# Twelve weight units of three output projections as 512 rows by 512 columns instead of 1024 by 256, in a float32 kernel of three blocks on one Trainium2 core

## The reference

```python
# first block: D_MIX = 1024
x = x + jnp.concatenate([o_gla, o_sgu], axis=-1) @ w_out[l]
h = rmsnorm(x, norm_mlp_g[l])
x = x + jnp.square(jax.nn.relu(h @ w_mlp1[l])) @ w_mlp2[l]
...
# second block: 2048 rows, ALPHA = 2 ** 0.25
mix = jnp.einsum("bse,ed->bsd", jnp.concatenate([y_ssm, y_attn], axis=-1), w_out.astype(h.dtype))
return layer_norm(ALPHA * h + mix, ln_g, ln_b)
...
# third block: 2048 rows
y = jnp.concatenate([y_conv, y_hgrn.astype(y_conv.dtype)], axis=-1)
h = h + y @ w_out[i].astype(y.dtype)
```

## Time and profile before

| | |
|---|---|
| median of 3 runs | 3835.29 us (3835.24 to 3836.01) |
| the profiled execution | 3835.1 us, span 3833.4 us |
| granted TensorE clock, mean over the span | 0.981 |
| TensorE matmuls | 20278, busy 95% of the span |
| VectorE, ScalarE, GpSimd busy | 59%, 45%, 15% |
| transfers | 191.40 MB read, 50.33 MB written, 63 GB/s |

### The profile page before, as it was taken

How to read it: one execution, slowest core, us unless ns; L and a number is a source line. 1 busy time by engine, 2 the same in 40 slices (tenths; PEclk the granted TensorE clock), 3 DMA queues, 4 the chain that set the end, 5 groups by cost and what they waited for, 6 DMA issues and landing times.

```text
span 3833.4 us, 48757 instructions
## 1 busy us (share of the span) xinstructions
PE 3642.6 (95%) x20278; PEld 3052.9 (80%) x20278; DVE 2272.0 (59%) x2931; ACT 1725.2 (45%) x2342; POOL 557.3 (15%) x437
## 2 busy tenths in 40 slices
PE   7999889999998998999999989989999999989998
PEld 6778878888876777777777768978888888778998
DVE  4445354456676766655565663468888878843332
ACT  4333244431124655566766772144555554542132
POOL 0001032200000444400000000012222222200001
PEclk9999999999998999999999999999999999999999
DMA  3012023342212011011111123121111111153111
GB/s 109 23 39 88 24 79 110 110 157 88 92 64 89 23 34 39 12 55 28 34 36 28 33 82 141 34 88 34 44 45 39 55 50 44 34 213 106 45 36 70
DMA packets 227392, 244.87 MB, mean 64 GB/s; under 512 B 10007, under 2 KB 190180, under 8 KB 227172
## 3 DMA queue, kind: packets, MB, share of 16 engines
q1 hardware_dynamic: 222391, 224.92, 18.0%
q10 hardware_dynamic: 4781, 16.84, 1.1%
HBM read 191.40 MB, written 50.33 MB: 63 GB/s over the span
## 4 chain that ended last, share of the span: by engine, by line
PE 81%; DVE 9%; ACT 6%; issue 2%; DMA 1%; POOL 1%; SPq 0%; ACTq 0%; DVEq 0%; POOLq 0%
PE pd L211 65%; PE pq L211 13%; PE pd L366 2%; PE pq L366 1%; DVE t L328 1%; DVE t L3457 1%; DVE t L3465 1%; ACT t L3062 1%; ACT t L320 1%; DVE t L3902 0%; ACT t L552 0%; DVE t L2400 0%; DMA yc_scratch<-t 0%; DVE t L560 0%; DVE t L2074 0%
## 5 line engine op out<-in xcount | busy, mean ns | idle before, releaser
L211 PE MATMUL pd<-t 128*128 128x512 f32 (+2 forms) x15104 | 2894.4, 352 | 50.3 <-DVE t L2592 8.7
L211 PEld LDWEIGHTS pd<-t 128*128 128x128 f32 x15104 | 2402.4, 191 | 482.1 <-issue 96.0
L211 PE MATMUL pq<-t 128*128 128x128 f32 (+5 forms) x3846 | 675.2, 335 | 60.5 <-DVE t L3938 16.7
L211 PEld LDWEIGHTS pq<-t 128*128 128x128 f32 (+2 forms) x3846 | 500.0, 181 | 183.0 <-issue 47.6
L320 ACT ACTIVATE t<-t 128x2048 fp32r<-128x2048 f32 (+3 forms) x133 | 212.6, 1599 | 633.8 <-PE pd L211 597.7
L328 DVE TENSOR_TENSOR t<-t 128x2048 fp32r<-128x2048 f32 (+3 forms) x133 | 257.5, 1936 | 180.8 <-ACT t L320 180.3
L1915 DVE TENSOR_TENSOR t<-pd,t 128x512 f32<-128x512 f32 x256 | 172.8, 689 | 103.3 <-PE pd L211 101.2
L2057 POOL TENSOR_TENSOR t<-t 128x2 f32<-128x2 f32 x8 | 10.5, 1307 | 1261.0 <-DVE t L3302 853.2
L3854 POOL TENSOR_TENSOR t<-t 128x512 f32<-128x512 f32 x56 | 96.4, 1722 | 593.8 <-ACT t L3798 316.6
L3185 DVE COPY t<-pd 128x512 f32<-128x512 f32 x64 | 44.2, 691 | 219.8 <-PE pd L366 219.8
L3465 DVE SCALAR_TENSOR_TENSOR t<-t 128x1024 f32<-128x1024 f32 x120 | 172.3, 1436 | 0.5
(11 more groups left out here) (336 smaller groups left out, 2996.6 us busy)
## 6 DMA issues: line engine op xcount, KB each, us to landing
t<-in_w_in_dram SPq DMA_DIRECT2D x97, 512.0 KB, 4.1
t<-in_w_out_dram SPq DMA_DIRECT2D x20, 1024.0 KB, 5.5
t<-in_w_in_dram SPq DMA_DIRECT2D x16, 1024.0 KB, 5.1
t<-in_w_mlp_dram SPq DMA_DIRECT2D x64, 256.0 KB, 3.4
u_scratch<-t SPq DMA_DIRECT2D x64, 256.0 KB, 2.4
t<-in_w_mlp_dram SPq DMA_DIRECT2D x16, 1024.0 KB, 5.0
t<-u_scratch SPq DMA_DIRECT2D x15, 1024.0 KB, 7.2
t<-in_x_dram SPq DMA_DIRECT2D x16, 512.0 KB, 9.2
```

What stands on the lines that cost most here:

```text
L211: ins = e.matmul(out, l, r, start=(first and j == 0), stop=(last and j == n - 1), skip_group_check=True)
```

## The change

Units 0 and 1 of products 1, o2b and o3c, units 2 and 3 of o2a and all four of o3b become units of 512 rows (`kq`, four blocks k) by 512 columns (`nh`). That makes twelve. In `pe_quarter` a tile is one position tile: 4 blocks k times three matmuls of 512 columns, 12 matmuls, and eight tiles in a unit. The sum over the 1024 rows no longer ends in one bank: the tile of `kq` 0 and the tile of `kq` 1 are each added to X by `dve_quarter`. The unit is still 1 MB and 2048 elements in each partition. In o2b the statistics of column blocks 0 and 1 are both taken after the additions of `kq` 1. `pe_proj` and `dve_proj` go; o2a keeps its unit 1 as it was. The diff is cut where a function goes as a whole.

```diff
     def proj_read(tag):
-        return lambda th: ("proj", tag, 3, 2 * th + 1)
+        return lambda th: ("proj", tag, 3, 4 * th + 3)
...
+    def pe_quarter(e, W, kg, kq, nh, v, tag, n):
+        u = pe_unit(e, W, [(nh * 512, 512)], k0=kg * 8 + kq * 4, k=4)
+        for tt in range(NT):
+            b = e.take(PD, "proj", tag, n, tt)
+            for k in range(4):
+                e.wait_ge(*at["HTh", v, kq * 4 + k, tt // 4])
+                e.wait_ge(*at["HTl", v, kq * 4 + k, tt // 4])
+                ins = mms(e, b[:, :], three(HTh[:, kq * 4 + k, tile(tt)], HTl[:, kq * 4 + k, tile(tt)],
+                                            u.h[:, k, :], u.l[:, k, :]), first=k == 0, last=k == 3)
+            ins.then_inc(*at.inc("pe", "proj", tag, n, tt))
+        pe_done(u)
+
+    def dve_quarter(e, X, nh, tag, n, t4, ready, alpha=None):
+        for tt in (2 * t4, 2 * t4 + 1):
+            o = X[:, tt, half(nh)]
+            b = PD.of("proj", tag, n, tt)
+            e.wait_ge(*at["proj", tag, n, tt])
+            e.wait_ge(*at[ready(tt)])
+            if alpha is None:
+                ins = e.tensor_tensor(o, b[:, :], o, ADD)
+            else:
+                ins = e.scalar_tensor_tensor(o, o, alpha, b[:, :], MUL, ADD)
+            ins.then_inc(*at.inc("dve", "added", tag, n, t4, free=("proj", tag, n, tt)))
+
+    QUARTERS = [(0, 0), (0, 1), (1, 0), (1, 1)]
...
     def pe_proj_led(e, W, kg, v, tag, turned_first=None):
-        for n in range(2):
-            u = pe_unit(e, W, [(n * 256, 256)], k0=kg * 8)
-            for t4 in range(4):
-                tm(e, u, 0, 256, [2 * t4, 2 * t4 + 1], v, "proj", tag, n, t4)
-            pe_done(u)
+        for kq in range(2):
+            pe_quarter(e, W, kg, kq, 0, v, tag, kq)
...
     def dve_norm_led(e, X, XN, v, tag, ready0, ready, gname, vacant):
-        for n in range(2):
+        for kq in range(2):
             dve_unit(e)
             for t4 in range(4):
-                dve_added(e, X, tag, n, t4, ready0)
+                dve_quarter(e, X, 0, tag, kq, t4, lambda tt: ("added", tag, 0, tt // 2) if kq else ready0(tt))
...
     def pe_sgu(e):
-        for n in range(2):
-            u = pe_unit(e, W, [(n * 256, 256)])
-            for t4 in range(4):
-                tm(e, u, 0, 256, [2 * t4, 2 * t4 + 1], "sgu", "proj", 1, n, t4)
-            pe_done(u)
+        for kq in range(2):
+            pe_quarter(e, W, 0, kq, 0, "sgu", 1, kq)
...
     def dve_out2(e):
-        dve_proj(e, X2, "o2a", lambda tt: ("x2", tt), ALPHA, begun=2, ahead=lambda e: load_b(e, 0))
+        for t4 in (2, 3):
+            dve_added(e, X2, "o2a", 0, t4, lambda tt: ("x2", tt), ALPHA)
+        dve_unit(e)
+        for t4 in range(4):
+            dve_added(e, X2, "o2a", 1, t4, lambda tt: ("x2", tt), ALPHA)
+        dve_unit(e)
+        for t4 in range(4):
+            dve_quarter(e, X2, 1, "o2a", 2, t4, lambda tt: ("x2", tt), ALPHA)
+        dve_unit(e)
+        for t4 in range(4):
+            if t4 == 2:
+                load_b(e, 0)
+            dve_quarter(e, X2, 1, "o2a", 3, t4, lambda tt: ("added", "o2a", 2, tt // 2))
         load_b(e, 1)
...
         for n in range(2):
             dve_unit(e)
             for p in range(4):
-                added(n, p)
+                dve_quarter(e, X2, 0, "o2b", n, p, lambda tt: ("added", *(("o2b", 0) if n else ("o2a", 3)), tt // 2))
+                if n == 1:
+                    e.wait_ge(*at["added", "o2b", 1, p])
+                    stats(0, p)
+                    stats(1, p)
...
     def pe_out2(e):
-        pe_proj(e, A["w_out_2"][0], 0, "o2a", "o2a", n0=1)
+        u = pe_unit(e, A["w_out_2"][0], [(256, 256)])
+        for t4 in range(4):
+            tm(e, u, 0, 256, [2 * t4, 2 * t4 + 1], "o2a", "proj", "o2a", 1, t4)
+        pe_done(u)
+        for kq in range(2):
+            pe_quarter(e, A["w_out_2"][0], 0, kq, 1, "o2a", "o2a", 2 + kq)
         pe_proj_led(e, A["w_out_2"][0], 1, "o2b", "o2b")
...
     def dve_out3(e):
-        dve_proj(e, X3, "o3b", lambda tt: ("x3", tt), ahead=lambda e: load_c(e, 0))
+        for n, (kq, nh) in enumerate(QUARTERS):
+            dve_unit(e)
+            for t4 in range(4):
+                if (n, t4) == (3, 2):
+                    load_c(e, 0)
+                dve_quarter(e, X3, nh, "o3b", n, t4, lambda tt: ("added", "o3b", n - 2, tt // 2) if kq else ("x3", tt))
...
     def pe_out3(e):
-        pe_proj(e, A["w_out_3"][0], 0, "o3b", "o3b")
+        for n, (kq, nh) in enumerate(QUARTERS):
+            pe_quarter(e, A["w_out_3"][0], 0, kq, nh, "o3b", "o3b", n)
```

More of the change, by code:

```diff
@@ L657, in act_fetch @@
             e.dma(tiles[k][:, :], src[k * 128:(k + 1) * 128, :], name, k)
-    def pe_proj(e, W, kg, v, tag, n0=0):
-        for n in range(n0, 4):
-            u = pe_unit(e, W, [(n * 256, 256)], k0=kg * 8)
-            for t4 in range(4):
-                tm(e, u, 0, 256, [2 * t4, 2 * t4 + 1], v, "proj", tag, n, t4)
-            pe_done(u)
+    def pe_quarter(e, W, kg, kq, nh, v, tag, n):
[21 more added lines that the diff above has]
+    QUARTERS = [(0, 0), (0, 1), (1, 0), (1, 1)]
     LED = [(2, 0), (2, 1), (3, 0), (3, 1), (2, 2), (2, 3), (3, 2), (3, 3)]
     def pe_proj_led(e, W, kg, v, tag, turned_first=None):
-        for n in range(2):
-            u = pe_unit(e, W, [(n * 256, 256)], k0=kg * 8)
-            for t4 in range(4):
-                tm(e, u, 0, 256, [2 * t4, 2 * t4 + 1], v, "proj", tag, n, t4)
-            pe_done(u)
+        for kq in range(2):
+            pe_quarter(e, W, kg, kq, 0, v, tag, kq)
         us = {}
@@ L726, in dve_norm_led @@
             dve_split_k(e, k, v, 1, gname)
[L728 to L735, removed]
     def dve_added(e, X, tag, n, t4, ready, alpha=None):
@@ L1448, in loaded_x @@
             return "x1", tt
-        for n in range(2):
+        for kq in range(2):
             dve_unit(e)
             for t4 in range(4):
-                dve_added(e, X1, 1, n, t4, loaded_x)
+                dve_quarter(e, X1, 0, 1, kq, t4, lambda tt: ("added", 1, 0, tt // 2) if kq else loaded_x(tt))
         dve_unit(e)
@@ L3291, in added, with stats @@
             e.wait_ge(*at["added", "o2b", n, p])
+            stats(n, p)
+        def stats(n, p):
             for tt in pair(p):
```

## The result

| | before | changed |
|---|---|---|
| median of 6 runs | 3835.34 us | 3820.88 us |
| lowest to highest | 3833.88 to 3836.58 | 3815.44 to 3823.87 |
| ratio, 95% interval | | 0.9959 (0.9949 to 0.9970) |
| the profiled execution | 3835.1 us, span 3833.4 | 3815.44 us, span 3813.7 |
| TensorE matmuls | 20278 | 19126, 1152 fewer |

The change saves 14.5 us by the medians, 0.38%; the ratio in the table, which is not the quotient of the medians, gives 0.41%, with an interval from 0.30 to 0.51%. 3819.9 us was forecast. The profiled execution is the fastest of its six, so of the 19.7 us between the two profiles only a part belongs to the change. Which part, the stretches tell.

The account below looks back on a forecast made before the run. TensorE was taken to bound the changed stretches: 1152 matmul pairs saving 13.3 ns each give 15.4 us, everything else costed at zero, so 3835.3 - 15.4 = 3819.9 us, range 3817.0 to 3827.8 us.

Parts of the forecast that it names:

- What bounds: Changed stretches: TensorE busy all the time at clock 1.00, VectorE about a third, so TensorE's savings reach the end.
- The durations: Changed units: a matmul takes 120.0 ns at 256 columns, 226.7 at 512, saving 13.3 ns per pair, 1.28 us a unit.
- The choice between 226.7 and 233.3: Changed units: of the down product's two 512-column speeds, 226.7 ns was taken for its same pairing of buffers.
- rival 1: All twelve units run at the slower cadence, 233.3 ns a matmul, saving 7.7 us, time 3827.6 us; chance 7%.
- Rival 2: Changed units: 512 columns cost 240 ns, so width alone brings nothing and the time stays at 3835 us; chance 3%.
- The skill's rule: Isolated matmul gap of N/2.4 ns plus 2.5 ns: a pair would save 2.5 ns, the twelve units 2.9 us.
- VectorE: Changed units: 48 more additions at 0.69 us, 33 us of work, covered by TensorE's time inside a unit.
- The banks: Four product heads: PSUM cover shrinks from 23.0 to 10.9 us, leaving margins of 1.1 to 1.8 us; costed at zero.
- rival 3: At the four heads TensorE starves for banks; slower by 0.2% from 5.8 us a head, example 3852 us; chance 2%.
- The clock: Low-clock stretches such as 480 to 490 us may lengthen or shorten as the program shifts; 2 us allowed either way.

Follow-up runs that it names:

- e_shift_w: Changed kernel with 32 bytes of padding in front of the weight rings: 3832.75 us, ratio 0.9991 to the kernel before.
- e_narrow: Changed kernel with each 512-column matmul of the twelve units made as two of 256 columns: 3839.03 us, ratio 1.0003 to the kernel before.
- e_head3: Changed kernel with three extra VectorE instructions of 2.3 us each ahead of the first addition of o3b: 3822.96 us in its one run.
- e_align64: Changed kernel with the small buffer lam widened from 4 to 12 floats, moving the stage buffers behind it: 3819.91 us, ratio 0.9954 to the kernel before.
- e_align128: Changed kernel with the small buffer lam widened from 4 to 28 floats, moving the stage buffers behind it: 3813.26 us, ratio 0.9937 to the kernel before.

## Why the prediction was right

The mechanism held: twelve units bounded by TensorE, 13.3 ns saved for each matmul less, nothing in return at the heads. That the median lies 1.0 us from the forecast is luck as far as the last microseconds go: single runs spread over 10 us.

- **What bounds.** TensorE was busy at full clock in the changed stretches before and after. Taking its time there as the end's time held.
- **The durations.** 120.0 and 226.7 ns, from the distance of evictions and not from the column of means, held to the last digit: 23.04 us a unit became 21.76. The means promised 196 us.
- **The choice between 226.7 and 233.3.** I took the faster row for being the same pairing of buffers, and gave the slower 7%. The choice was right, and the reason only half: e_shift_w pairs the same buffers and is slow. What decides is the place of the two operands, which rival 1 named as the only difference, and the pairing was a good guide because it kept the place.
- **Rival 2, width alone brings nothing**, got 3%. It was wrong here, yet its outcome is what the twelve units show with the rings 32 bytes on, at 0.456 ns a column and not at its 240 ns for 512. The rows from which I excluded it excluded it for this placement only. And what I read as a fixed 13.3 ns of every matmul is fixed only while the operands start at the same place.
- **The skill's rule.** The Trainium skill ("TensorE: Matmul & The Clock Gate", section "Back-to-back issue gap") would have had 2.9 us for the change by its isolated gap. e_narrow measures the width by itself at 17 us (ratio 1.0003 against 0.9959) and by its cadences at 15.4. The trace and the runs do not agree with the rule for these float32r matmuls.
- **VectorE.** 2302.7 us busy instead of 2272.0, 30.7 more where 33 were counted. None of it shows in the time. In o2b's second unit TensorE kept its cadence.
- **The banks.** The margins were forecast at 1.1, 1.8, 1.4 and 1.8 us and measured 1.1, 1.8, 1.6 and 1.8. The wait of e_head3 was 5.58 us against 5.5. What rival 3 left out is the clock: the stalled head lost 8.4 us, so its prices for a late addition are too low.
- **The clock.** I allowed 2 us either way for what shifts at stage ends. That was too little for a single execution: the eleven runs of the changed kernel lie between 3815.4 and 3825.8, and its first profile was 4.4 us better in untouched stretches. The medians, 3820.88 and 3822.53, are 1.0 and 2.6 us above the forecast. In the two pairs of kernels whose buffers had been moved, the change came with 5 to 6 us more than its own stretches show; I had costed everything outside them at zero.

## What to carry to other kernels

Take the cost of a matmul from the distance between two evictions in a full stretch, at both widths, and for the pair of buffers that it will really use: the profile's mean durations were off by a factor of more than ten for the saving. Before narrowing or widening, look whether the stationary and the moving operand start at the same place within 512 bytes; here moving the stage buffers by 224 bytes was worth as much as the rewriting of twelve units. When tiles get shorter, count the banks in microseconds and compare with what the evicting engine does at each head, and price a stall at more than its length.

## What the runs showed of the hardware

- **The place of the operands within 512 bytes (or 256) sets the cadence of float32r matmuls.** Same place: 226.7 ns for 512 columns, 120.0 for 256, once the stream has settled. Different place: 232.5 to 233.3 for 512 (the padded rings 32 bytes past it; TL 224 bytes short of it in the changed kernel, 192 in e_align64, 128 in e_align128), and 116.7 for 256 (only the 32 bytes were tried there). Width pays in the first case and does nothing in the second. Why, the traces don't show. The Trainium skill ("TensorE: Matmul & The Clock Gate", section "Step-by-step: what each phase is for") says that the next weights and the running matmul are read by two ports, and that loading doesn't take bandwidth from the matmul; the runs here show that the stream's speed depends all the same on where the two lie against each other. Whether the ports have to do with it is not shown.
- **Below 256 columns the cadence hardly falls.** In the trace of the kernel before, most spacings of 128-column matmuls at full clock are 108 to 112 ns, against 120 for 256.
- **A stall costs more than its length.** After the wait of 5.58 us in e_head3 the granted clock was 0.50 from 3511.5 to 3516.0 us, and the head lost 8.4 us.
- **The clock at gaps.** Stages with waits on TensorE differ by some microseconds between executions of the same program; the tail of the first block's projection had a mean granted clock of 0.95 in one profile and 0.84 in the other, and TensorE was busy for 23.5 and 26.1 us with the same 158 matmuls.
